# Seven products instead of eight blocks in the squared-relu MLPs of a 512-token, eight-stage transformer kernel

## The reference, cut to what matters

```python
D_FF = 4 * D_MODEL
def _sqrelu_mlp(x, w_up, w_down):
    return jnp.square(jax.nn.relu(x @ w_up)) @ w_down
x = _layernorm(DEEPNORM_ALPHA * x + _sqrelu_mlp(x, ffn_w_up[i], ffn_w_down[i]), ln_ffn_g[i], ln_ffn_b[i])
```

## Time and profile before

| what | us |
| --- | --- |
| median of 3 runs (2498.62 to 2499.23) | 2498.78 |
| the profiled execution, own time | 2496.68 |
| its span in the trace | 2494.8 |
| PE busy | 2479.5 |
| VectorE busy | 1289.2 |
| POOL busy | 1177.0 |
| ScalarE busy | 898.9 |

### The profile page before, as it was taken

The page is one execution under the profiler, slowest core; times in us unless marked ns, Lnnn a source line. Parts: engine busy times, 40 slices in busy tenths (PEclk is TensorE's granted clock), DMA queues, the critical chain, the costliest instruction groups (busy, mean ns, idle before and its releaser), DMA issues.

```text
span 2494.8 us, 32165 instructions
## 1 busy us (share of the span) xinstructions
PE 2479.5 (99%) x12101; PEld 2061.7 (83%) x12101; DVE 1289.2 (52%) x1939; ACT 898.9 (36%) x1262; POOL 1177.0 (47%) x879
## 2 busy tenths in 40 slices
PE   9999999999999999999999999999999999999998
PEld 8778888888888888888888888888888888888887
DVE  6557344457576444435333566666233143466666
ACT  4445222244565222224334333333232233433332
POOL 4224444444333444444332566664533434566664
PEclk9999999999999999999999999999999999999999
DMA  6113322323212233223221333333222221322332
GB/s 185 61 51 106 101 87 97 101 75 112 73 64 88 98 101 101 86 99 102 68 69 67 102 101 101 101 102 121 91 85 85 85 85 68 107 97 100 99 102 78
DMA packets 166627, 230.87 MB, mean 93 GB/s; under 512 B 11254, under 2 KB 128124, under 8 KB 166396
## 3 DMA queue, kind: packets, MB, share of 16 engines
q1 hardware_dynamic: 166524, 229.44, 28.0%
HBM read 227.32 MB, written 2.10 MB: 92 GB/s over the span
## 4 chain that ended last, share of the span: by engine, by line
issue 43%; PE 29%; POOL 27%; ACT 0%; POOLq 0%; DVE 0%
POOL w_lo L734 27%; PE banks L794 6%; PE banks L796 6%; PE banks L795 6%; PE banks L1592 2%; PE banks L1594 2%; PE banks L1593 2%; PE banks L1097 1%; PE banks L1051 1%; PE banks L964 0%; PE banks L1102 0%; PE banks L1133 0%; PE banks L1135 0%; PE banks L1134 0%; PE banks L1032 0%
## 5 line engine op out<-in xcount | busy, mean ns | idle before, releaser
L734 POOL TENSOR_TENSOR w_lo<-w_raw,w_hi 128x512 fp32r<-128x512 f32 (+1 forms) x820 | 1108.3, 1383 | 1297.8 <-ACT w_hi L1828 1288.4
L1828 ACT ACTIVATE w_hi<-w_raw 128x2048 fp32r<-128x2048 f32 x204 | 390.4, 1914 | 598.3 <-PE banks L807 254.0
L794 PE MATMUL banks<-h_hi,w_hi 128*128 128x512 f32 x1448 | 567.3, 392 | 0.3 <-POOL w_lo L734 0.3
L796 PE MATMUL banks<-h_hi,w_lo 128*128 128x512 f32 x1448 | 563.5, 389 | 0.0
L795 PE MATMUL banks<-h_lo,w_hi 128*128 128x512 f32 x1448 | 563.5, 389 | 0.0
L2401 DVE TENSOR_TENSOR x_residual<-x_residual,banks 128x512 f32<-128x512 f32 x311 | 213.1, 687 | 238.0 <-PE banks L807 197.0
L794 PEld LDWEIGHTS banks<-h_hi,w_hi 128*128 128x128 f32 x1448 | 271.9, 188 | 61.9 <-issue 4.2
L796 PEld LDWEIGHTS banks<-h_hi,w_lo 128*128 128x128 f32 x1448 | 271.8, 188 | 56.9
L795 PEld LDWEIGHTS banks<-h_lo,w_hi 128*128 128x128 f32 x1448 | 271.9, 188 | 56.8 <-issue 1.2
L805 PE MATMUL banks<-w_hi,act_hi 128*128 128x512 f32 x664 | 259.1, 390 | 0.7 <-POOL w_lo L734 0.7
L807 PE MATMUL banks<-w_hi,act_lo 128*128 128x512 f32 x664 | 258.4, 389 | 0.0
(11 more groups left out here) (316 smaller groups left out, 3858.4 us busy)
## 6 DMA issues: line engine op xcount, KB each, us to landing
w_raw<-in_ffn_w_in SPq DMA_DIRECT2D x44, 1024.0 KB, 5.1
w_raw<-in_ffn_w_up SPq DMA_DIRECT2D x32, 1024.0 KB, 5.3
w_raw<-in_ffn_w_down SPq DMA_DIRECT2D x32, 1024.0 KB, 4.9
w_raw<-in_ret_w_in SPq DMA_DIRECT2D x24, 1024.0 KB, 5.2
w_raw<-in_ffn_w_out SPq DMA_DIRECT2D x36, 512.0 KB, 4.5
w_raw<-in_diff_w_qkv SPq DMA_DIRECT2D x12, 1024.0 KB, 5.2
w_raw<-in_fox_w_in SPq DMA_DIRECT2D x12, 1024.0 KB, 5.3
w_raw<-in_ret_w_out SPq DMA_DIRECT2D x8, 1024.0 KB, 5.1
```

The costliest lines, as they stand in the source:

```text
L734: nc.gpsimd.tensor_tensor(m.w_lo[:, sl, at], m.w_raw[:, sl, at], m.w_hi[:, sl, at].bitcast(F32), ALU.subtract)\
L794: mm(out, hi, x[0][:, k, :], start=k == 0, stop=False)
L796: last = mm(out, lo, x[0][:, k, :], start=False, stop=k == kc - 1)
L1828: m.nc.scalar.activation(m.w_hi[:, sl, 0:width], m.w_raw[:, sl, 0:width], ACT.Copy).then_inc(m.sem("w_hi_ready"), 1)
```

## The change

NR = 13 groups (1 to 13) of each squared-relu stage go by the seven products too. Group 0 stays as it was, and so do the last two. On each engine:

- **PE** (`pe_relu_products`): 42 matmuls for the 48 of `down`. The order is INTO_22, SUM_5, SUM_2, INTO_11, DIFF_3, DIFF_4, SUM_AB in bank pairs 2, 0, 4, 2, 0, 6, 2. SUM_2 and DIFF_4 stay in PSUM over the stage and accumulate there. The other five are evicted in each group. Banks 0 and 1 are also those of the up block: SUM_5 waits for both squares of the next group, and the next up block for the eviction of DIFF_3.
- **VectorE** (`step`): both squares of the next group (relu times the bank, one operand in PSUM), evictions 0 and 1, corners_low and two mixes, evictions 2 and 3, the third mix, eviction 4, three weight mixes, mixes_low. Ten folds come in the last group.
- **ScalarE** (`step`): hi of corners, mixes and weight mixes in place of the hi square. The split of a down unit waits for the weight mixes.
- **POOL** (`relu_mlp`): `joined_low`, three pieces, after each down unit.
- **SyncE**: a down unit comes as two transfers of 512 KB.

The core of the diff (`product_operands`, `pe_product` and `dve_weight_mixes` were parts of the swiglu code; `square`, `mix`, `corners_low` and their like follow it):

```diff
+NR = G1 - 3
...
+RELU_ORDER = (INTO_22, SUM_5, SUM_2, INTO_11, DIFF_3, DIFF_4, SUM_AB)
+RELU_BANKS = (2, 0, 4, 2, 0, 6, 2)
+RESIDENT = {SUM_2: 4, DIFF_4: 6}
+RELU_ROTATING = tuple(n for n, product in enumerate(RELU_ORDER) if product not in RESIDENT)
+ROTATING = len(RELU_ROTATING)
+RELU_FOLDS = sorted(FOLDS, key=lambda fold: fold[1] not in RESIDENT)
+RELU_FOLDED = {bank: max(n for n, fold in enumerate(RELU_FOLDS) if fold[1] == product) + 1 for product, bank in RESIDENT.items()}
+RELU_ACC = KC + len(FOLDS) + KC
...
+                done(f"{t}.d{g - 1}", *range(PRODUCTS))
...
+            in_blocks([f"{t}.d{g}" for g in gs], down, i * 2 + 2, i)
...
+    def relu_mlp(t):
+        with pool.Fori(0, (NR - 1) // 2) as i:
+            for e in range(2):
+                gs = range(1 + e, NR, 2)
+                n = INDEX[f"{t}.d{gs[0]}"]
+                split_low(i * 4 + n, n % 2, 2048)
+                joined_low(t, [g - 1 for g in gs], i)
+                split_low(i * 4 + n + 1, (n + 1) % 2, 2048)
...
+            pe.wait_ge(*m.upto(f"{t}_squared", along(i, [2 * g + j - 1 for g in gs])))
+            if gs[0] >= 3:
+                pe.wait_ge(*m.upto(f"{t}_evicted", along(i, [ROTATING * (g - 3) + ROTATING - 1 for g in gs])))
...
+def pe_relu_products(m, pe, t, gs, i=None):
+
+    names = [f"{t}.d{g}" for g in gs]
+    operands = product_operands(m, slot(names), 2 * (gs[0] % 2))
+
+    def evicted(more):
+        pe.wait_ge(*m.upto(f"{t}_evicted", along(i, [ROTATING * (g - 1) + more for g in gs])))
+
+    pe.wait_ge(*m.upto(f"{t}_a_lo", along(i, [2 * g + 2 for g in gs])))
+    for n, product in enumerate(RELU_ORDER):
+        if n < 4:
+            pe_weights(m, pe, names, i, (1, 2, 3, 4)[n])
+        else:
+            pe.wait_ge(*m.upto(f"{t}_w_mix_lo", along(i, [3 * g + n - 6 for g in gs])))
+        if n == 0 and gs[0] > 1:
+            evicted(0)
+        elif n == 1:
+            pe.wait_ge(*m.upto(f"{t}_squared", along(i, [2 * g + 4 for g in gs])))
+        elif n in RELU_ROTATING and n:
+            evicted(RELU_ROTATING.index(max(k for k in range(n) if RELU_BANKS[k] == RELU_BANKS[n])) + 1)
+        elif product in RESIDENT and gs[0] == 1:
+            pe.wait_ge(*m.upto(f"{t}_acc", KC))
+        resident = product in RESIDENT
+        pe_product(m, operands[product], RELU_BANKS[n], not resident or gs[0] == 1, not resident or gs[-1] == NR)
...
+        if groups == G1 and which == 0 and n in (0, 2):
+            pe.wait_ge(*m.upto(f"{t}_acc", KC + RELU_FOLDED[TAIL_BANK[n]]))
...
+    def step(gs, i=None):
+        after_it = [g + 1 for g in gs]
+        split_blocks(gs, i)
+        relu(after_it, 0, i)
+        joined_high(gs, i)
+        relu(after_it, 1, i)
+        if gs[0] < NR:
+            corners_high(after_it, i)
+        else:
+            high(NR + 1, 0), high(NR + 1, 1)
         act_split(m, act, after([f"{t}.d{g}" for g in gs]), i)
-
-    up([0])
-    up([1])
-    down([0])
+        if gs[0] < NR:
+            mixes_high(after_it, i)
...
+def dve_weight_mixes(m, dve, t, names, count):
+
+    sl, v = slot(names), m.nc.vector
+    raw = m.w_raw[:, sl, 0:2048].rearrange("p (a b) -> p a b", a=4)
+    pairs, done = raw.rearrange("p (a c) b -> p a c b", c=2), m.sem(f"{t}_w_mixed")
+    v.tensor_tensor(m.joined[:, 0:1024].rearrange("p (a b) -> p a b", a=2), pairs[:, :, 0, :], pairs[:, :, 1, :], ALU.subtract).then_inc(done, 1)
+    v.tensor_tensor(m.joined[:, 1024:1536], raw[:, 2, :], raw[:, 1, :], ALU.add).then_inc(done, 1)
+    dve.wait_ge(*m.upto(f"{t}_w_mixed", count))
+    v.tensor_tensor(raw[:, 0:4:3, :], raw[:, 2:4, :], raw[:, 0:2, :], ALU.add).then_inc(done, 1)
...
+    def square(gs, j, i=None):
+        dve.wait_ge(*m.upto("blocks_done", block_done(i, [f"{t}.u{g}" for g in gs], j)))
+        dve.wait_ge(*m.upto(f"{t}_relu", along(i, [2 * g + j + 1 for g in gs])))
+        if gs[0]:
+            dve.wait_ge(*m.upto(f"{t}_a_hi", along(i, [2 * g for g in gs])))
+            dve.wait_ge(*m.upto(f"{t}_a_lo", along(i, [2 * g for g in gs])))
+        v.scalar_tensor_tensor(out=m.square[:, j, :], in0=b[j][:, :], scalar=0.0, in1=m.relu[:, j, :], op0=ALU.max, op1=ALU.mult)\
+            .then_inc(s(f"{t}_squared"), 1)
...
+    def evict(gs, k, i=None):
+        n = RELU_ROTATING[k]
+        product, bank = RELU_ORDER[n], m.banks[:, RELU_BANKS[n]:RELU_BANKS[n] + 2, :]
+        into = {INTO_22: (1, 1), INTO_11: (0, 0)}.get(product)
+        out = quadrant(m, into) if into else m.relu_sums[product]
+        dve.wait_ge(*m.upto("blocks_done", block_done(i, [f"{t}.d{g}" for g in gs], n)))
+        if gs[0] > 1:
+            dve.wait_ge(*m.upto(f"{t}_evicted", along(i, [ROTATING * (g - 2) + k + 1 for g in gs])))
+        elif into:
+            dve.wait_ge(*m.upto(f"{t}_acc", KC))
+        if gs[0] == 1 and not into:
+            v.tensor_copy(out, bank).then_inc(s(f"{t}_evicted"), 1)
+        else:
+            v.tensor_tensor(out, out, bank, ALU.add).then_inc(s(f"{t}_evicted"), 1)
+
+    def fold(first, end):
+        for n, (q, product, sign) in list(enumerate(RELU_FOLDS))[first:end]:
+            earlier = [k for k in range(n) if RELU_FOLDS[k][0] == q]
+            if earlier:
+                dve.wait_ge(*m.upto(f"{t}_acc", KC + earlier[-1] + 1))
+            bank = RESIDENT.get(product)
+            x, more = quadrant(m, q), m.relu_sums[product] if bank is None else m.banks[:, bank:bank + 2, :]
+            v.tensor_tensor(x, x, more, ALU.add if sign > 0 else ALU.subtract).then_inc(s(f"{t}_acc"), 1)
+
+    def step(gs, i=None):
+        after_it = [g + 1 for g in gs]
+        more = gs[0] < NR
+        square(after_it, 0, i), square(after_it, 1, i)
+        evict(gs, 0, i), evict(gs, 1, i)
+        if more:
+            corners_low(after_it, i), mix(after_it, 0, i), mix(after_it, 1, i)
+        else:
+            low(NR + 1, 0), low(NR + 1, 1)
+        evict(gs, 2, i), evict(gs, 3, i)
+        if more:
+            mix(after_it, 2, i)
+        evict(gs, 4, i)
+        if more:
+            weight_mixes(after_it, i), mixes_low(after_it, i)
...
+    step([NR])
+    dve.wait_ge(*m.upto("blocks_done", BLOCK[f"{t}.d{NR}", PRODUCTS - 1]))
+    dve.wait_ge(*m.upto(f"{t}_evicted", ROTATING * NR))
+    fold(0, 6)
+    square([G1 - 1], 0), low(G1 - 1, 0)
+    fold(6, 8)
+    square([G1 - 1], 1), low(G1 - 1, 1)
+    fold(8, len(FOLDS))
+    end(by_tile(TAIL_ADDS, dve_last_groups(m, dve, t, G1, True)), folded_complete(KC))
```

More of the change, by code:

```diff
@@ L439, in memory @@
     m.mix_hi, m.mix_lo = (a[:, 4:7, :].rearrange("p a b -> p (a b)")[:, 0:1280] for a in (m.act_hi, m.act_lo))
-    m.mix, m.joined = tok[:, 0:1280], tok[:, 1280:2816]
+    m.joined, m.mix, m.relu_mix = tok[:, 0:1536], tok[:, 1536:2816], view(5120, 1280)
+    m.relu_sums = {product: view(2048 + 1024 * n, 1024, 2) for n, product in enumerate((SUM_5, DIFF_3, SUM_AB))}
     m.sums = [view(at, 1024, 2) for at in (2048, 3072, 5120, 6144, 7168)]
@@ new lines, in pe_product @@
+def pe_product(m, operands, bank, begin=True, end=True):
+    mm, (x, w) = m.nc.tensor.matmul, operands
+    for tile in range(2):
+        out, (hi, lo) = m.bank[bank + tile], (a[:, P * tile:P * tile + P] for a in x)
+        mm(out, hi, w[0], start=begin, stop=False)
+        mm(out, hi, w[1], start=False, stop=False)
+        last = mm(out, lo, w[0], start=False, stop=end)
+    last.then_inc(m.sem("blocks_done"), 1)
+def pe_relu_products(m, pe, t, gs, i=None):
[19 more added lines that the diff above has]
+        pe_product(m, operands[product], RELU_BANKS[n], not resident or gs[0] == 1, not resident or gs[-1] == NR)
@@ L1577, in pe_products @@
+def pe_products(m, pe, t, gs, i=None):
+    names = [f"{t}.d{g}" for g in gs]
+    operands = product_operands(m, slot(names), 2 * (gs[0] % 2))
     pe_weights(m, pe, names, i)
@@ L1589, in pe_products @@
             pe.wait_ge(*m.upto(f"{t}_evicted", along(i, [PRODUCTS * g + before for g in gs])))
[L1590 to L1595, removed]
+        pe_product(m, operands[product], PRODUCT_BANKS[n])
 def pe_swiglu(m, pe, t, beside, beside_at=7):
@@ L2131, in act_relu_mlp @@
+    relu([1], 0), relu([1], 1), corners_high([1])
+    act_split(m, act, [f"{t}.u2"])
+    mixes_high([1])
     if t == "ffn0":
@@ L2795, in dve_relu_mlp @@
+    for j in range(2):
+        square([0], j), low(0, j)
     if t == "ffn0":
         dve_rope(m, dve, "diff", 2)
-    up([1])
+    square([1], 0), square([1], 1)
     dve.wait_ge(*m.upto(f"{norm}_done", TT))
-    down([0])
-    with dve.Fori(0, (G1 - 4) // 2) as i:
-        for e in range(2):
-            up(range(2 + e, G1 - 2, 2), i)
-            down(range(1 + e, G1 - 3, 2), i)
-    up([G1 - 2])
-    down([G1 - 3])
-    up([G1 - 1])
-    last_groups()
+    corners_low([1])
+    for part in range(3):
+        mix([1], part)
```

215 lines of the change are left out of this document (122 added, 93 removed).

## The result

| | before | after |
| --- | --- | --- |
| median, us | 2498.70 (4 runs, 2498.20 to 2499.23) | 2552.68 (4 runs, 2549.15 to 2555.99) |
| ratio, 95% interval | | 1.022 [1.0207, 1.0233] |
| the profiled execution, own time | 2496.68 | 2555.99 |
| its span | 2494.8 | 2553.7 |
| mean granted clock | 0.999 | 0.990 |

A forecast was written before the change was run, and what follows sets the result against it. TensorE, busy 99% of the span, was taken as the bound. Per stage -17.7 + 37.2 (stops, groups 1 to 12) + 1.2 (group 13) + 1.5 (tail) = +22.2 us; both +44.4, so 2543 us, range 2510 to 2560.

The forecast's parts named there:

- the mechanism: Products of each group: POOL's pieces hold three VectorE operations, delaying the eviction SUM_AB needs; 2516 to 2550 us, chance 0.80.
- PE's work: Each group: 42 matmuls replace 48, 1.36 us less, 17.7 us per stage and 35.4 in both.
- SUM_5: Second product of a group: PE waits for both squares, losing 0.2 us plus 0.1 at the restart.
- The three held operations: VectorE's corners_low and two mixes before INTO_11's eviction wait 3.6 us for POOL; PE stops 2.7 us at SUM_AB.
- "Granted clock 1.00", the rival at 0.03: PE's clock expected to stay 1.00; rival: it falls at each stop, 1.35 us in 24 groups, 2575 us, chance 0.03.
- The start: Group 0's eight additions stand behind corners_low and three mixes, 2 to 5 us; at worst some tenths lost, nothing taken.
- Group 13: Last group by products: two lows replace the three operations; about 1.2 us lost with both stops.
- The tail: End of a stage: ten VectorE folds come in between, so PE waits 1.5 us more for a low.
- Loads: Down units come as two transfers, landing 4.5 us after issue and by 6, wanted at 14; costs nothing.
- Waits that stay small (0.11): Rival: VectorE's three operations before INTO_11's eviction hardly wait, kernel faster; 2474 us with no wait, chance 0.11.
- POOL keeps the port the whole unit (0.04): Rival: VectorE waits until POOL has done all four up-unit pieces; period 1.2 us longer, 2572 us, chance 0.04.

The follow-up runs named there:

- the weights first: Changed kernel with evictions 2 and 3 ahead of the first two activation mixes, and weight mixes ahead of eviction 4: 2483.54 us, 0.9939 of the kernel before.
- both runs with fills: Changed kernel with six, or two, zero-weight matmuls put ahead of SUM_AB in groups 1 to 12: 2535.25 us with six, 2536.66 us with two.
- the run with two fills: Changed kernel with two zero-weight matmuls put ahead of SUM_AB in groups 1 to 12: 2536.66 us, ratio 1.0155 to the kernel before.

## Why the prediction was right, and where it was wrong

Forecast 2543 us in a range of 2510 to 2560, slower with 0.87; measured 2552.68. The sign, the place and the mechanism were right; of the 54 us about 38 are the mechanism forecast, about 16 come of a step that said nothing would happen. That the number came within 10 us is in part luck: the mechanism was over-estimated by some 7 us and the clock left out, and the two errors offset each other. The bounds worked out for the mechanism were 2516 to 2550, and the time lies above them; only the 10 us that the stated range adds, for which no reason was given, take it in.

*PE's work.* 42 matmuls for 48, as counted. Not seen as a gain in this kernel, since the stops are longer; with the weights first it is.

*SUM_5.* Forecast a stop of 0.2 and 0.1 at the restart. PE at the start of group 4's products:

```profile
318.55 0.39 PE L1611 MATMUL banks<-w_hi,act_hi 128*128 128x512 f32 x1
...
319.69 0.39 PE L1613 MATMUL banks<-w_hi,act_lo 128*128 128x512 f32 x1
320.13 0.50 PE L1611 MATMUL banks<-w_hi,act_hi 128*128 128x512 f32 x1
320.47 0.39 PE L1612 MATMUL banks<-w_lo,act_hi 128*128 128x512 f32 x1
```

0.44 to SUM_5's first matmul and 0.34 to its second, where two times 0.2267 would be: 0.2 and 0.1 lost.

*The three held operations.* Forecast waits of 1.1, 1.26 and 1.26 and a stop of 2.7; from start to start the stop at 329.38 is 2.31 (2.54 less 0.23). Right in place and number: POOL's up unit starts 4.4 us after the group's first product (322.96, against 318.55 in the rows above) where 4.3 was worked out (from terms that add up to 6.3 and not 6.4, which changes it by 0.1), and corners_low and both mixes are 1.70 apart. The size was a little off: I added a whole piece, 1.26, and the operation's 0.60 to 1.86 per turn. The turn is 1.70, and the earlier trace rows had it already, 1468.06 to 1469.76. Two turns, 0.32 us per group. So without the clock the period is 23.2 and not 23.5, as both runs with fills show in groups 3 to 12, and the sum +37 in place of +44; they measured +36.8 and +38.2.

*"Granted clock 1.00", the rival at 0.03.* **This step failed.** I took from the earlier trace rows that the clock stays through stops up to 1.0 us and gave the fall in a stop of 2.7 us a chance of 0.03, although the same paragraph said that such a stop is nearer to the end of the trace than anything else in it. It fell after stops as short as 1.82 us, and after each of 2.12 and more. The rival's price, 1.35 us in 24 groups, was near in size (1.6 us) and too high in number (14 of 24), since a fall shortens the next stop. The Trainium skill (TensorE: Matmul & The Clock Gate, "Why this matters for your kernels") warns of idle gaps between bursts of matmuls. The trace agrees that a gap can bring a fall, but not on its length: here gaps of 1.82 to 2.15 us did, shorter than the one that the page names. A chance of 0.03 was too low, since nothing in the trace before had a stop over 1.0 us with work on both sides.

*The start.* I took nothing. In the first stage PE waited 0.8 us for an addition of group 0, which stood behind corners_low and three mixes, the third of them 1.53 us for 256 elements; from relu to relu 1.2 us. The two runs with fills show both outcomes, 0 and 1.2.

*Group 13* gained 0.5 us (its relu rows 21.29 apart) where +1.2 - 1.36 was forecast. *The tail*, from the last relu to the last h_lo of the stage, took 30.73 us against 30.00: 0.7 where I had 1.5. *Loads*: a down unit's halves landed 4.2 us after issue, nothing waited for them.

*Waits that stay small (0.11).* Fell, by the rows above. That it looked at the right thing the runs show: with one or two of the three operations out of the way the stop is 0.6 us or less and the time within 5 us of the kernel before.

*POOL keeps the port the whole unit (0.04).* Fell: VectorE's operations and POOL's pieces alternate in every group, the unit takes 6.35 us. The Trainium skill (SBUF — State Buffer, "Who interferes with whom") has the lock exclusive for a whole instruction. The trace agrees: each of the four pieces is an instruction of its own, and VectorE gets its turn between two of them.

The difference to the run with two fills adds up. The 14 falls of 1.6 us, less 0.32 in each of the 12 stops that follow one, make 18.6 us, the start 1.2. The profiled execution is 21.4 above (2555.99 against 2534.64). The rest, 1.6 us, is a fifteenth fall, which no stop precedes. It stands in the forgetting attention, after the second squared-relu stage, behind 20 matmuls of 8 columns that follow each other without a stop from 1231.92 on; the matmuls of 256 columns after them stand 0.21 us apart instead of 0.12:

```profile
1233.17 0.81 PE L1534 MATMUL banks<-gate_f,ones 128*128 128x8 f32 x6
...
1235.13 0.41 PE L833 MATMUL banks<-w_hi,h_hi 128*128 128x256 f32 x1
```

The run with the weights first has a fall at the same place of the program (1162.4), the other six traces have none there, the kernel before among them. So it does not come with the change each time; whether the change makes it likelier is not shown. Why four of the short stops, the first two in each stage, had a fall and the ten later ones none stays open.

## What to carry to other kernels

Before VectorE is given operations on SBUF alone in front of an eviction that TensorE waits for, look at what POOL does then: each such operation costs a turn of POOL's piece and its own time (here 1.70 us for 0.6), and one moved behind the eviction was worth 52 us here. Where TensorE must stand, the stop can have a second price in the clock, so look at the distance of the matmuls after it, and not at the wait alone. Once the stop is gone, ask for the next in line: only with the weight mixes earlier as well did fewer matmuls become less time.

## What was not expected of the hardware

Stops of TensorE of 2.12 to 2.15 us, one in 48 us and with one of 1.82 between, were each enough for the lower clock. It came 0.5 to 0.7 us after work began again and stayed for 3.4 us. Of the stops of 1.81 to 1.87 us four of 14 had it, of the 24 of 1.39 to 1.70 with two fills none. Without any stop it came in two of the eight traces behind 20 matmuls of 8 columns. So a program can be faster by 16 us for computing more: two useless matmuls per group.
